# Three moves of issue order in a four-layer kernel: the recurrence's end, the start of a run of quarters, and two small products of the third layer

## The reference, cut to what matters

```python
def mlstm_post(h, o_pre, g):                       # layers 0 and 1, after both directions are added
    h = h * lax.rsqrt(jnp.mean(h * h, axis=-1, keepdims=True) + EPS)
    ...
    return (h * jax.nn.sigmoid(o_pre.astype(jnp.float32))).astype(o_pre.dtype)

def swiglu(h, w_gu, w_down):                       # feed-forward, every layer
    gate, up = jnp.split(h @ w_gu, 2, axis=-1)
    return (jax.nn.silu(gate) * up) @ w_down

def _rope(x, cos, sin):                            # layers 2 and 3: queries and keys
    ...
    return jnp.stack([x0 * c - x1 * s, x0 * s + x1 * c], axis=-1).reshape(x.shape)
...
mod = (c_act @ w_mod[l] + b_mod[l])[:, None, :]    # modulation
```

## Time and profile before

| | |
|---|---|
| median of 3 runs | 2070.97 us (2070.21 to 2073.69) |
| the profiled execution's own time | 2070.35 us |
| its span, first to last instruction | 2068.9 us |
| PE busy | 1993.1 us, 96% of the span |
| DVE, ACT, POOL busy | 1397.4, 1041.2, 425.4 us |
| mean granted TensorE clock | 0.998 of full speed |
| chain that ended last | PE 67%, DVE 17%, ACT 6%, POOL 4% |

### The profile page before, as it was taken

One profiled execution on the slowest core, in us unless ns is written; L12 is line 12 of the kernel. 1 busy time (PEld: TensorE's weight loads), 2 busy tenths in 40 slices (PEclk: granted clock), 3 DMA queues, 4 the chain that ended last, 5 costly groups with the idle time before them and its releaser, 6 DMA issues.

```text
span 2068.9 us, 32856 instructions
## 1 busy us (share of the span) xinstructions
PE 1993.1 (96%) x12934; PEld 1681.7 (81%) x12934; DVE 1397.4 (68%) x2361; ACT 1041.2 (50%) x1942; POOL 425.4 (21%) x324
## 2 busy tenths in 40 slices
PE   6999999999999899999999999999999999999999
PEld 4777677988997787899976567798898777779999
DVE  4394657967987776655564765795898866676555
ACT  3444644542553655654455783453255256555443
POOL 1000416521541003100010341751253100000000
PEclk9999999999999999999999999999999999999999
DMA  9642522538448824556453102244832732115563
GB/s 338 233 142 82 183 67 78 191 113 277 148 154 261 299 96 138 184 173 214 139 190 120 62 17 86 96 165 136 260 101 88 241 106 68 62 61 164 164 214 112
DMA packets 276745, 311.65 MB, mean 151 GB/s; under 512 B 6128, under 2 KB 260208, under 8 KB 269424
## 3 DMA queue, kind: packets, MB, share of 16 engines
q1 hardware_dynamic: 271888, 304.90, 45.3%
q10 hardware_dynamic: 4704, 4.65, 0.7%
HBM read 308.48 MB, written 1.05 MB: 150 GB/s over the span
## 4 chain that ended last, share of the span: by engine, by line
PE 67%; DVE 17%; ACT 6%; POOL 4%; issue 3%; DMA 2%; ACTq 0%; DVEq 0%; POOLq 0%
PE bank L781 65%; DVE weights_low L1551 3%; DVE weights_low L1948 3%; PE bank L790 2%; ACT weights_high L2359 2%; DVE scratch L1543 1%; DVE yT L1543 1%; DMA modulation_slots<-p_modulation_rows 1%; DVE input_low L1543 1%; DVE modulation_slots L1577 1%; DMA parameter_columns<-p_columns 1%; DVE big L2194 1%; DVE big L1543 1%; POOL weight_slots L697 1%; DVE xT L1543 1%
## 5 line engine op out<-in xcount | busy, mean ns | idle before, releaser
L781 PE MATMUL bank<-input_high,weights_high 128*128 128x256 f32 (+1 forms) x2336 | 748.9, 322 | 18.1 <-DVE scratch L1984 9.1
L781 PE MATMUL bank<-input_high,weights_low 128*128 128x256 f32 (+1 forms) x2336 | 735.1, 316 | 0.0
L781 PE MATMUL bank<-input_low,weights_high 128*128 128x256 f32 (+1 forms) x2336 | 713.8, 317 | 2.6 <-DVE input_low L1543 2.6
L1551 DVE TENSOR_TENSOR weights_low<-weight_slots,weights_high 128x1024 fp32r<-128x1024 f32 (+2 forms) x344 | 386.9, 1164 | 187.0 <-ACT weights_high L2359 186.7
L781 PEld LDWEIGHTS bank<-input_high,weights_high 128*128 128x128 f32 x2336 | 439.7, 188 | 77.0 <-issue 25.3
L781 PEld LDWEIGHTS bank<-input_high,weights_low 128*128 128x128 f32 x2336 | 439.7, 188 | 33.1
L781 PEld LDWEIGHTS bank<-input_low,weights_high 128*128 128x128 f32 x2336 | 433.6, 188 | 39.7 <-DVE input_low L1543 6.4
L2359 ACT ACTIVATE weights_high<-weight_slots 128x1024 fp32r<-128x1024 f32 (+2 forms) x348 | 314.4, 950 | 149.7 <-PE bank L781 136.7
L1948 DVE TENSOR_TENSOR weights_low<-weight_slots,weights_high 128x512 fp32r<-128x512 f32 x216 | 233.9, 1102 | 24.7 <-ACT weights_high L2639 22.0
L781 PE MATMUL bank<-hidden_high,weights_high 128*128 128x256 f32 (+1 forms) x704 | 238.4, 339 | 0.6 <-DVE weights_low L1551 0.4
L781 PE MATMUL bank<-hidden_low,weights_high 128*128 128x256 f32 (+1 forms) x704 | 237.3, 337 | 0.0
(11 more groups left out here) (279 smaller groups left out, 2758.4 us busy)
## 6 DMA issues: line engine op xcount, KB each, us to landing
weight_slots<-w_gu SPq DMA_DIRECT2D x44, 1024.0 KB, 5.3
weight_slots<-ffn_w_in SPq DMA_DIRECT2D x44, 1024.0 KB, 5.2
modulation_slots<-p_modulation_rows SPq DMA_DIRECT2D x64, 512.0 KB, 4.8
modulation_slots<-mod_w SPq DMA_DIRECT2D x32, 1024.0 KB, 5.1
modulation_slots<-w_mod SPq DMA_DIRECT2D x28, 1024.0 KB, 6.2
weight_slots<-w_in SPq DMA_DIRECT2D x24, 1024.0 KB, 8.8
weight_slots<-w_down SPq DMA_DIRECT2D x16, 768.0 KB, 5.1
weight_slots<-ffn_w_out SPq DMA_DIRECT2D x16, 768.0 KB, 4.7
```

The costliest lines, as they stand in the source:

```text
L781: return pe.matmul(o, w, r, start=start, stop=stop, skip_group_check=shared)
L1551: tt(m.w_low[:, g % 2, c], m.ring[:, g % SLOTS, c], m.w_high[:, g % 2, c].bitcast(F32), ALU.subtract).then_inc(m.low_made.sem, 1)
```

## The change

The computation is the same; only places in the issue order move.

In `mlstm` on ACT, `modulate` (the copy of the modulation row) stands right behind the intra copy, ahead of `normalised`; the norm of head 1 moves from step 7 (behind `normalised`) to step 8, behind that copy and ahead of `normalised`. On PE, the turn of head 1 moves from ahead of the last inter product to behind it. In `by_quarters` on DVE, the add of the first P1 moves ahead of the low parts of steps 5 and 6, in all four runs. In `even_projection` on PE, `even_swap(1)` moves behind tile 5, and the swap of step 12 behind the scores of that step.

```diff
@@ tensor_program, mlstm
             if e == 9:
-                for j in range(2):
-                    turn_head(L, j)
+                turn_head(L, 0)
             if 2 <= e:
                 output_of(e - 2, *units[e - 2])
+            if e == 9:
+                turn_head(L, 1)
             modulate("mlstm", L, e)
@@ tensor_program, even_projection
                 even_head_sums(1)
                 even_tokens(1)
+            elif e == 5:
                 even_swap(1)
...
-            if 6 <= e and e - 2 in EVEN_NORMED:
+            if 6 <= e and e - 2 in EVEN_NORMED and e != 12:
                 even_swap(EVEN_NORMED.index(e - 2))
             if e in (8, 10, 12):
...
                 even_scores(e // 2 - 4)
+            if e == 12:
+                even_swap(EVEN_NORMED.index(e - 2))
@@ vector_program, by_quarters
-        for j in range(FIRST_SPLIT, LOOK):
-            low_quarters(L, r, j)
+        low_quarters(L, r, FIRST_SPLIT)
...
-            low_quarters(L, r, j + LOOK)
+            if j:
+                for s in range(FIRST_SPLIT + 1 if j == 1 else j + LOOK, j + LOOK + 1):
+                    low_quarters(L, r, s)
@@ scalar_program, mlstm
                 i.then_inc(m.intra_out.sem, 1)
+            modulate("mlstm", L, e)
             if e == 1:
                 high_weights(m.outp[L][1])
+            elif e == 8:
+                head_norm(1)
             if e >= 2:
                 normalised(e - 2)
-            if e in (5, 7):
-                head_norm((e - 5) // 2)
+            if e == 5:
+                head_norm(0)
             if e == 8:
                 for k in MIXED[0:2]:
                     high(k)
-            modulate("mlstm", L, e)
```

## The result

The changed kernel takes 2079.12 us (median of 7 executions, 2075.94 to 2082.36) against 2070.97 of the kernel before on the same chip. The ratio is 1.0034, with a 95% interval of 1.0024 to 1.0045, so the loss is clear of the noise. The prediction was 2073.5 with a range up to 2077.0. The profiled execution of the changed kernel took 2075.94 us, the fastest of the seven, with a span of 2074.4.

A forecast was written before the change was run, and what follows sets the result against it. PE was taken as the bound, busy 1993.1 of 2068.9 us, so reordering gains only at its stalls. Quarters +0.9 and +2.9, swap -1.8, recurrence +0.8 made +2.8 us: 2073.5 forecast, range 2067.5 to 2077.0.

The forecast's parts named there:

- The order terms: Effects of the moved issue order: quarters +0.9 and +2.9, third layer's swap -1.8, recurrence's end +0.8, sum +2.8 us.
- the four quarter runs: Quarters, layers 0 and 2: POOL's chain starts later, delaying P3; first runs +0.9 us together, second runs +2.9.
- The seven later stalls: Layer 2's second quarter run: PE waits seven times for the add of P5; a late chain isn't caught up.
- The first swap: Third layer, swap of tile 10's keys: moved behind tile 5, PE's 1.79 us wait goes, -1.8 us.
- the late ones: Third layer's later swaps: PE's gain in one wait is stood in the next, 0 us, bounds -0.5 and +0.2.
- In layer 1 the first tile: Recurrence's end, layer 1: ACT is through 0.8 us later, PE's first tile starts near 835.45 instead of 834.94, +0.5 us.
- In layer 0 ACT: Recurrence's end, layer 0: ACT bounds, reaches 253.25, 0.4 us later; first tile at 252.8, next head's turn late, +0.3 us.
- rival (c): Longer PE gaps before P3 and head 1's turn bring two low-clock stretches, +3.4 us on top: 2076.9; chance 0.20.
- the stalls of 1.93 and 0.87 us: First quarter run, PE's waits before P6 and P3: they brought no low-clock stretch, used as evidence against the clock loss.
- (a): The first P1's add comes earlier and nothing else is late: -3.8 us together, 2066.9; chance 0.12.
- (b): POOL's chain is late only in the first quarter runs, second runs meet fewer low parts: -0.7 us, 2070.0; chance 0.20.
- the signs listed: P6 1.1 us earlier, P3 stall 2.4, new second-run stall 1.5 to 2, 1.79 wait gone, ACT's second scaling without wait.

The follow-up runs named there:

- the P5 edit: Kernel before, with the add of P5 put ahead of the low part issued with the P2 before it: 2063.87 us, ratio 0.9960.
- low part 5 ahead: Quarters' change alone on the kernel before, but low part 5 stays ahead of the first P1's add, only low part 6 behind: 2074.93 us, ratio 1.0010.
- the first filled version: Quarters' change alone on the kernel before, plus 36 and 28 unread passes before the first P3 of each run: 2077.66 us, ratio 1.0027.
- the changed kernel's repeat: The changed kernel run again, nothing altered, beside its filled versions on one chip: mean 2079.57 us against 2071.84 for the kernel before.
- the best one: Kernel before, with the add of P5 ahead of the low part issued with P2, and layer 2's first swap behind tile 5: 2062.80 us, ratio 0.9946.

## Why the prediction was wrong

**The order terms were right.** By the table of differences the four quarter runs cost +0.48, +1.34, about +0.4 (its +3.07 less the 1.6 that a low stretch cost behind the other P3) and +1.36, together 3.6 where 3.8 was forecast, and by the mechanism named: POOL's start late by 1.75 us in the second runs (2.93 to 4.68) for the 1.77 forecast, and 7.61 us from there to P3. The prediction took from the Trainium skill (SBUF — State Buffer, "SBUF: two separate sides") that low parts and sums lock each other out and the chain stays at 7.67 us. The trace agrees: the chain is 7.61 us, and the sums beside the low parts take 1.61 us again. The seven later stalls of layer 2's second run did not take the delay up: PE is 5.7 us late behind its first P3 and 5.6 at 1600. The first swap gave -2.05 for -1.8, the late ones nothing where no low stretch lies behind them (the kernel with the turn filled). In layer 1 the first tile came 0.55 later for +0.5. In layer 0 ACT was through at 253.29, the forecast being 253.25, and the first tile came at 253.04 for 252.8; what the order costs there lies under a low stretch in this trace. In the three kernels with the turn filled, whose recurrence has the same order and no low stretch at 252, the tiles behind come 0.3 us later than before, for the +0.3 forecast. So the traces give the order 3.6 - 2.0 + 0.9 = 2.5 us, and the sum said +2.8. The times give a little more. With both stalls filled, at a mean clock 0.001 above that of the kernel before, the change costs 2.6 us by the medians and 2.0 by the means, and 3.4 by the means brought to the same clock at 1.4 us for 0.001.

**The step that failed is the clock.** The sum has no term for it, and rival (c), which had the mechanism, was held back with a chance of 0.20 and two stretches of low clock. In the mean over the executions the changed kernel has 0.9950 where the kernel before has 0.9981: 0.0031, which by the measured 1.4 us for 0.001 is 4.3 us. With the order's 3.4 it makes 7.7, the measured difference of means in that group (2079.57 and 2071.84). This is a division of the difference and no second test, for the 1.4 comes from means of the same group; with the 1.43 of the 171 other executions the parts are 4.4 and 3.4, 7.8 together. Rival (c) had +3.4 for two stretches, 1.7 each. A stretch like the one behind 528 takes 0.0008 off the mean clock, so 0.0031 stands for nearly four more in each execution, at some 1.1 us each. The one behind 528 cost 1.59 at once, of which 0.4 was made up again. So rival (c) had the mechanism, half the number of stretches, and a size that is an upper bound; its chance of 0.20 was too low.

Two steps of the working led there. First, "the stalls of 1.93 and 0.87 us, five microseconds apart, brought none" was read from one execution. In the profiled execution of the version with the P5 edit and the swap, PE stands 1.97 us before the same P6, and the windows ahead of 360.5 and behind it are:

```profile
356.00:360.50 4.50, 2.53 (x21) 2.33 (x20) 4.07 (x6) 3.93 (x9) 1.95 (x2) 1.00 0.90 346
360.50:364.00 3.50, 3.50 (x20) 3.50 (x19) 3.35 (x3) 1.36 (x5) 3.34 (x3) 0.54 1.03 378
```

So such a stall brings a low stretch in some executions and none in others. The kernel with the swaps alone, whose quarters are those of before, has one too, from 363.7 on, behind a stall of 1.91 us. One trace cannot exclude it, and the executions of the kernel before differ in their clock: they range from 2068.58 us to 2077.07 in the first group, with clocks from 1.0 to 0.996. Second, the working counted each new stall as time that PE stands and put nothing behind it, though longer stalls in five of the places were its own result. The number of stalls tells little here: behind the first 20 us, the profiled executions have six of over 1.7 us before (11.7 us in all) and seven after (14.6), with two and four low stretches. The long gap that the Trainium skill (TensorE: Matmul & The Clock Gate, "HAM oscillation") puts behind a fall of the clock was not there: low stretches came behind stalls of 1.83 to 2.50 us, and in the traces of the filled kernels none came behind a filled one.

**Rivals (a) and (b)** fall: the chain was late in all four runs. Of the signs listed, all came as told (P6 1.03 earlier, stall 2.44, new stall 1.83, swap wait gone, ACT without a wait), and none of them spoke of the clock.

The traces of all 18 profiled executions together say where the low stretches came. Each count is of the places in these traces at which one began, out of the places there are:

```
place                              before's order  changed, unfilled  filled
first runs, behind P6 or P3        4 of 12         5 of 8             0 of 10
second runs, behind the first P3   0 of 14         3 of 8             0 of 10
layer 0, behind the turn           3 of 7          6 of 6             0 of 5
layer 1, behind the turn           4 of 7          5 of 6             0 of 5
layer 2, behind the late swaps     0 of 9          7 of 9             -
```

The columns go by the order at each place, and filled is the stall before the first P3 or the turn. The first two rows leave out the kernel with low part 5 ahead and the P5 edit on the changed kernel, and the first also the kernel with the stall before P6 filled. At every place the change made them more frequent, also at the late swaps, which the forecast put at nothing and no experiment filled: there 1.36 and 0.70 us of stall became 0.29 and 1.77. The rises add up to 2.9 stretches for an execution of the changed kernel, against nearly four by the mean clock. These are one trace a kernel, so each single count is rough.

What stays open: in layer 0's recurrence the clock also fell in kernels whose recurrence is that of before (the first filled version, the swaps alone, low part 5 ahead), and the turn had a stall of 2.14 us before the change as well, so the 3.2 us that filling it gives are not all the change's. The same holds for layer 1, where the kernel before had its stretch. And the granted clock is not all that differs between executions: in the profiled one of the changed kernel's repeat, PE is busy through 100 us near the end at a granted clock of 1.00 and makes 852 matmuls in them, where it makes 859 in the kernel before. From 1900 on that is 1.5 us, and no run here tells its cause.

## What to carry to other kernels

A stall of PE costs twice: its own length, and the low clock that may follow. Here new or longer stalls of 1.8 to 2.5 us went with some 3 us of order and some 4 of clock. When a working ends in new stalls of that size, put the clock into the sum, and read it from the mean of many executions, not from one trace. Before moving work ahead of an operation that another engine starts from, look for the operation that ends the stall and move that instead: one low part of each item put behind the add of P5 was worth 8 us, where moving the add of P1 lost 5 to 6. A filler is measured against the wait at every place where its line runs: the same 18 passes fitted in layer 0 and cost 1.5 us in layer 1.

## What the runs showed of the hardware that was not expected

- PE's clock fell to half behind single stalls of 1.83, 1.97, 2.44 and 2.50 us with full work behind them, at a cost of up to 1.6 us a stretch (1.59 behind 528) and some 1.1 on the mean.
- It does so in some executions and not in others: the same program gives 1.0 and 0.996. With products of 128x128 that nothing reads in the stall, no low stretch came behind it in any trace here: 3.2 us gained for each kind of stall in the changed kernel, and nothing that could be measured in the best one.
- A filler that outlasts the wait gives back the gain: 36 passes at 0.11 us held P3 up by 1.3 us, and 18 in a wait of 0.52 us held a head's turn up by 1.5.
